# A two-block transformer kernel: linear heads in pairs on the two row halves, rotary queries of two heads in one unit, no engine barriers, early weight sums, idle products in the router

## The chip, the cores and the metric

One core of a Trainium2 chip. The metric is the device time of one execution in microseconds (us), lower is better. Everything is float32.

## What is computed

512 tokens of width 1024 pass two blocks.

Block one: a modulated norm and a gated feed-forward (width 2816), a mixer of 16 heads of 64 (8 stick-breaking, 8 softmax with forget gates and normalized queries and keys), and a second feed-forward.

Block two puts 16 meta tokens in front, so 528 positions:

```
z = rmsnorm(h) @ w_in                      # q, k, v, r, decay input, q_lat, kv_lat, k_rope
linear heads (4): chunks of 64 tokens; q_e = q exp(b), b = running sum of log decay in the chunk
   att = causal(q_e (k exp(-b))^T);  o = att v + q_e S;  S <- decay S + (k exp(b_last - b))^T v
   o <- o / rms(o) * gain * silu(r)
softmax heads (4): q = rmsnorm(q_lat) @ w_qb, 128 plain and 64 rotary values for each head
   scores = q k^T + rope(q_r) rope(k_r)^T, causal by chunk; softmax; times v
h <- h + concat(heads) @ w_out
router: one of 8 groups, in it the best 2 of 8 experts; h <- h + sum of gated expert outputs
```

The experts (64, of 6 MB each) end in a last norm.

## The kernel before

TensorE, VectorE (DVE), ScalarE (ACT) and SyncE (SP, which issues all transfers) each run one hand-ordered program; semaphores tie them. Weights come through six slots of 2 MB; `freed[s]` and `filled[s]` guard them. PSUM is eight banks.

**Barriers.** `phase_end` (L489) drains an engine and waits for all four; it stands ahead of both feed-forwards and of the second block (2, 8, 10). TensorE only reports there.

**Feed-forward** (`ffn`, L854, L897): each weight item goes through seven products of sums and differences of weights and tokens. Products one and two take plain weights and tokens; the third needs two weight sums (`gate_up_sum`, L1950 to L1962) and two token sums (`token_sum`, L1968 to L1977) of VectorE. VectorE makes the two weight sums of item 0 first, then two token sums, and so on (`ffn`, L2036). The token sums need the normed tokens that ScalarE scales (L1543).

**Mixer.** In the loop over heads TensorE turns the probabilities of head h (L977), makes scores of head h+1 (L968), the output of head h (`head_out`, L995) in bank 6, and half of a later pair's projections (`first_half` L944, `second_half` with `values` L950), whose banks are 6 and 7. Projections into bank 6 wait for `s_o`, the copy of the head's output by VectorE (L2170). The last two heads cover part of the output product, the rest (L1035) follows in eight tiles; VectorE adds each (L2231), ScalarE squares it (L1528), VectorE adds the squares (L1933).

**Norm of block two** (`norm(3)`): VectorE multiplies a tile with the inverse root (L1939), ScalarE with the gain (L1546), TensorE projects it (L1106).

**Linear heads.** Units (L1106 to L1120) project; `chunk_update` (L1156) makes the update of a chunk, VectorE the state (L2295). A head sits on 64 rows: heads 0 and 2 on the lower, 1 and 3 on the upper half. For each head in turn TensorE runs `gla_out` (L1177, then L1180 on the head's rows), `gla_scores` of the next head (L1163), and between them `mla_unit`s, three for each softmax head: query (L1197), rotary query (L1199, 64 columns), key (L1204). `gla_sum` (L1186) sums squares, ScalarE makes the inverse root (L1758, L1759), VectorE scales (L2310, L2311). VectorE turns the rotary queries (L2321 to L2326), masks scores (L2305). ScalarE copies plain queries and keys (L1747, L1749).

**Softmax heads.** 16 units, head by head, query tiles 0, 1, 2, 3. TensorE turns the probabilities of unit n (L1279, L1281), makes scores of n+2 (L1259 to L1262), then the output of n (L1291, L1293), which waits for ScalarE's copy of the turned tiles (L1779).

**Router and experts.** After the logits (L1318) VectorE picks experts in some 30 small steps while TensorE waits for `s_M`; two products (L1355, L1356) give ranks; VectorE norms the last rows (L2381, it stands ahead of the ranks' use) and marks the rows of the first four experts (L2434). `pick_first(b)` (L1373) gathers the rows of block b, ScalarE copies them (L1851), TensorE turns them (L1380), ScalarE copies (L1855), then `gate_up` (L1410) and `down` (L1430). SP issues in order: weights for block 3 when gate and up of block 0 are done (L707), a part of block 2 when down of block 0 is done (L741), then those of block 4, and so on in a loop.

`w_qb` is loaded by one transfer (L691) into slot 1, where `decay_product` (L1128) waits for it.

## Time and profile before

| | |
|---|---|
| median of 3 runs | 2441.39 us (2439.96 to 2443.12) |
| the profiled execution | 2439.12 us, span 2437.3 us |
| TensorE busy, granted clock | 89%, 0.957 |
| VectorE, ScalarE busy | 40%, 21% |
| moved from HBM | 546 MB, in the experts' part at 427 to 430 GB/s |

The span is the time between the first and last recorded instruction. PE is TensorE, PEld its weight loads; the clock is the share of full speed granted (0.50 is the 1.2 GHz level, 1.00 the 2.4 GHz one). One float32 matmul is two records. An idle time is followed by the instruction that ended it.

### The profile page before, as it was taken

Reading aid. Unit: us, or ns where it says so; the run is one execution under the profiler, and the core shown is the slowest. Engines: PE = TensorE matmul, PEld = TensorE weight load, DVE = VectorE, ACT = ScalarE, POOL = GpSimd, SP = SyncE. Lnnn points to the kernel's source line nnn. Section 1 sums busy time; section 2 is a strip of 40 time slices with the busy share of each in tenths; the row PEclk is TensorE's granted clock in tenths of the full one; section 3 lists DMA queues with packets and bytes.
Section 4 is the critical chain, followed back from the end, with each engine's and each line's share of the span. In section 5 each row is a group of like instructions: output and inputs, shape, how many; then the busy total and the mean of one; then the engine's idle time right before and its main releaser. Section 6 shows DMA issues by size and latency. Waiting matters only on the chain.

```text
span 2437.3 us, 34407 instructions
## 1 busy us (share of the span) xinstructions
PE 2158.9 (89%) x14427; PEld 1511.1 (62%) x14427; DVE 974.4 (40%) x1725; ACT 509.0 (21%) x1052; POOL 0.2 (0%) x4
## 2 busy tenths in 40 slices
PE   7999999999999999999999998777777777777776
PEld 4888888666564888888754554444444444444443
DVE  4777753145443543453223525322232222222223
ACT  3111100244323111110221422211111111111112
POOL 0000000000000000000000000000000000000000
PEclk9999999999999999999999999988998989998998
DMA  7565721411202224212401044999999999999997
GB/s 280 187 228 174 250 95 48 104 37 42 96 1 69 69 70 151 70 66 78 148 14 69 1 190 181 427 427 428 429 427 430 428 429 429 427 430 428 429 429 298
DMA packets 150550, 549.06 MB, mean 225 GB/s; under 512 B 9376, under 2 KB 102832, under 8 KB 124736
## 3 DMA queue, kind: packets, MB, share of 16 engines
q1 hardware_dynamic: 150464, 547.83, 57.1%
q8 instruction: 65, 1.06, 0.2%
q14 instruction: 21, 0.17, 0.0%
HBM read 545.71 MB, written 2.10 MB: 225 GB/s over the span
## 4 chain that ended last, share of the span: by engine, by line
PE 62%; DMA 30%; DVE 4%; ACT 1%; issue 1%; SPq 1%; ACTq 0%; PEldq 0%; DVEq 0%; PEld 0%
DMA slots<-in_expert_w_up 27%; PE ps L854 18%; PE ps L897 11%; PE ps L1410 8%; PE ps L944 4%; PE ps L1342 2%; PE ps L1035 2%; PE ps L1120 2%; PE ps L950 2%; DMA slots<-in_w_mod 2%; PE ps L968 1%; PE ps L1115 1%; PE ps L1118 1%; PE ps L977 1%; DMA slots<-in_expert_w_down 1%
## 5 line engine op out<-in xcount | busy, mean ns | idle before, releaser
L1410 PE MATMUL ps<-slots,xT 128*32 128x256 f32 x4032 | 292.8, 454 | 188.9 <-DMA slots<-in_expert_w_up 169.4
L1410 PEld LDWEIGHTS ps<-slots,xT 128*32 128x32 f32 x4032 | 158.3, 130 | 311.3 <-issue 176.8
L854 PE MATMUL ps<-hT,slots 128*128 128x256 f32 x1408 | 314.1, 381 | 6.5 <-ACT hT L1543 3.6
L854 PEld LDWEIGHTS ps<-hT,slots 128*128 128x128 f32 x1408 | 267.8, 191 | 46.5 <-ACT tmp L1564 4.5
L854 PE MATMUL ps<-slots 128*128 128x256 f32 x1056 | 238.0, 382 | 5.6 <-DVE slots L1972 5.6
L854 PEld LDWEIGHTS ps<-slots 128*128 128x128 f32 x1056 | 201.7, 192 | 33.8 <-issue 6.3
L2514 DVE COPY hT<-ps 128x128 f32<-128x128 f32 x64 | 18.5, 289 | 418.1 <-PE ps L1417 418.1
L2520 DVE TENSOR_TENSOR big<-ps,big 128x512 f32<-128x512 f32 x128 | 88.3, 691 | 219.0 <-PE ps L1445 219.0
L1831 ACT ACTIVATE xT<-ps 32x256 f32<-32x256 f32 x256 | 96.2, 376 | 259.5 <-PE ps L1430 257.3
L1430 PE MATMUL ps<-slots,hT 128*32 128x256 f32 x2040 | 123.3, 381 | 30.0 <-DVE hT L2514 29.5
L1825 ACT ACTIVATE big<-ps 32x256 f32<-32x256 f32 x128 | 48.0, 375 | 392.4 <-PE ps L1410 391.6
L1445 PE MATMUL ps<-xT,hT 128*128 128x512 f32 x256 | 123.5, 618 | 3.5 <-DVE big L2520 1.9
L897 PE MATMUL ps<-big,slots 128*128 128x256 f32 x528 | 116.6, 379 | 0.0
L1362 PEld LDWEIGHTS ps<-xT,big 128*128 128x128 f32 x960 | 108.3, 192 | 6.2 <-issue 6.2
L1362 PE MATMUL ps<-xT,big 128*128 128x128 f32 x960 | 111.2, 277 | 0.0
L897 PEld LDWEIGHTS ps<-big,slots 128*128 128x128 f32 x528 | 100.3, 190 | 13.6
L1430 PEld LDWEIGHTS ps<-slots,hT 128*32 128x32 f32 x2040 | 71.7, 109 | 58.1 <-issue 33.5
L944 PE MATMUL ps<-hT,slots 128*128 128x512 f32 x240 | 105.8, 596 | 0.0
L2033 DVE SCALAR_TENSOR_TENSOR xT<-ps,small,xT 128x256 f32<-128x256 f32 x56 | 27.0, 483 | 169.1 <-PE ps L897 169.1
L1445 PEld LDWEIGHTS ps<-xT,hT 128*128 128x128 f32 x256 | 39.5, 188 | 80.9 <-DVE big L2520 64.8
L1528 ACT ACTIVATE tmp<-xT 128x512 f32<-128x512 f32 (+1 forms) x32 | 20.2, 635 | 290.3 <-DVE xT L2033 254.5
L944 PEld LDWEIGHTS ps<-hT,slots 128*128 128x128 f32 x240 | 44.8, 190 | 54.6 <-issue 54.5
(381 smaller groups left out, 2562.1 us busy)
## 6 DMA issues: line engine op xcount, KB each, us to landing
slots<-in_expert_w_gate SPq DMA_DIRECT2D x63, 2048.0 KB, 18.4
slots<-in_expert_w_up SPq DMA_DIRECT2D x63, 2048.0 KB, 22.8
slots<-in_expert_w_down SPq DMA_DIRECT2D x63, 2048.0 KB, 24.7
slots<-in_w_mod SPq DMA_DIRECT2D x18, 2048.0 KB, 11.5
slots<-in_w_gate SPq DMA_DIRECT2D x22, 1024.0 KB, 5.5
slots<-in_w_up SPq DMA_DIRECT2D x22, 1024.0 KB, 8.1
slots<-in_w_down SPq DMA_DIRECT2D x8, 2816.0 KB, 10.2
slots<-in_w_in SPq DMA_DIRECT2D x24, 512.0 KB, 5.6
```

Of the source, the lines that this page charges most:

```text
L854: last = mm(bank[:, g], lhs[:, g, k], rhs[:, k], start=(first and g == 0 and k == 0), stop=(k == 3), skip_group_check=True)
L897: last = mm(bank, lhs[:, f], rhs[:, f], start=(first and f == 0), stop=(f == N_ITEM - 1), skip_group_check=True)
L944: last = mm(ps[:, bank, :], pair_w[p][:, k, m, :], hT[:, k, META:TOK], start=(k == 0), stop=(k == KC - 1))
L950: last = mm(ps[:, bank, t * P:(t + 1) * P], hT[:, k, META + t * P:META + (t + 1) * P], pair_w[p][:, k, 2, :], start=(k == 0), stop=(k == K ...
L1035: last = mm(ps[:, bank, :], wo[f // 4][:, f % 4, d * P:(d + 1) * P], oT[:, f, :], start=(f == f0), stop=(f == f1 - 1))
L1120: last = mm(ps[0:m, b, :], w2(it)[:, k, c0:c0 + m], hT[:, k, META:TOK], **flags)
L1362: last = mm(flat[:, 2048 + k * P:2048 + (k + 1) * P], u2[:, t, k * P:(k + 1) * P], hot[:, t, :], start=(t == 0), stop=(t == NT - 1))
L1410: last = mm(ps[at:at + CAP, j, 0:256], xsT[:, k, i * CAP:(i + 1) * CAP], w[g][k][:, 256 * h:256 * (h + 1)], start=(k == 0), stop=(k == KC ...
L1430: last = mm(ps[g * CAP:(g + 1) * CAP, 2 + j, 0:256], hid[j][:, c, :], w[c][:, g * 256:(g + 1) * 256], start=(c == 0), stop=(c == 3))
L1445: mm(ps[:, 4 + n % 2, :], gate_rows[:, n // 2, :], ys[:, n % 2 * 512:(n % 2 + 1) * 512], start=True, stop=True).then_inc(s_cmb, 1)
L1831: last = av(ys[i * CAP:(i + 1) * CAP, g * 256:(g + 1) * 256], ps[g * CAP:(g + 1) * CAP, 2 + i % 2, 0:256], ACT.Copy)
L2520: v.tensor_tensor(h2[:, t, g * 512:(g + 1) * 512], ps[:, 4 + g, :], h2[:, t, g * 512:(g + 1) * 512], ALU.add).then_inc(s_sum, 1)
```

## The change

- The barriers are gone.
- Mixer: head outputs go to bank 3; waits for head copies become waits for the copies that really share a bank, and a turn waits for the copy of the head before.
- The four weight sums of item 0 of the second feed-forward are made in the last four output tiles of the mixer.
- `norm(3)`: VectorE multiplies with root and gain at once, ScalarE does nothing.
- `w_qb` is laid out with all plain columns first, by four transfers; the rotary queries of two heads are one unit of 128 columns, 10 units in place of 12; tables and keys are doubled on the upper rows.
- Linear heads in pairs: matmuls of the two heads alternate; chunk updates too; two buffers each for masks, squares and roots.
- Query tiles of the softmax heads in the order 3, 0, 2, 1.
- Router: six products of 512 columns whose result nobody reads; the first rows of block 1 are picked after gate and up of block 0, those of block 2 after those of block 1.

In the diff, removed lines of the functions printed above are left out where a new version stands.

```diff
@@ -279,12 +278,12 @@
 o2 = hT[:, :, :].rearrange("p k t -> p (k t)")[:, 0:8 * SEQ].rearrange("p (c t) -> p c t", c=8)
-attS = eb[:, 0, :].rearrange("p (b c) -> p b c", b=4)
-osq = eb[:, 1, :]
-sil = tmp[:, 0, 0:SEQ]
-orst = tmp[:, 1, 0:SEQ]
+attS = [eb[:, j, :].rearrange("p (b c) -> p b c", b=4) for j in range(2)]
+osq = [extra[:, SEQ * j:SEQ * (j + 1)] for j in range(2)]
+sil = [extra[:, SEQ * (2 + j):SEQ * (3 + j)] for j in range(2)]
+orst = [extra[:, SEQ * (4 + j):SEQ * (5 + j)] for j in range(2)]
...
-qr = ring[0][0:ROPE, 2048:4096].rearrange("p (h t) -> p h t", h=GH)
+qr = ring[0][:, 2048:3072].rearrange("p (h t) -> p h t", h=GH // 2)
@@ -449,12 +448,13 @@
 def halves(ap):
...
-NU = 3 * GH
+MLA_PARTS = [(p, kind, 2 * p + j) for p in range(GH // 2) for kind, j in ((0, 0), (1, 0), (2, 0), (0, 1), (2, 1))]
+NU = len(MLA_PARTS)
...
 def mla_unit_out(n):
...
-    h, kind = n // 3, n % 3
-    return (s_mb, h + 1) if kind == 1 else (s_mtc, 2 * h + (1 if kind == 0 else 2))
+    p, kind, h = MLA_PARTS[n]
+    return (s_mb, p + 1) if kind == 1 else (s_mtc, 2 * h + (1 if kind == 0 else 2))
@@ -470,27 +470,18 @@
+MLA_UNITS = [(h, t) for h in range(GH) for t in (3, 0, 2, 1)]
...
 def mla_at(un):
-    return 1024 * (un % 2) + (512 - META if un % NT == NT - 1 else 0)
+    return 1024 * (un % 2) + (512 - META if MLA_UNITS[un][1] == NT - 1 else 0)
...
 def mla_z(un):
...
-    t = un % NT
+    _, t = MLA_UNITS[un]
...
-JOINED = (19, 22)
...
-def joined_count(n):
-    return 4 * (JOINED.index(n) + 1) if n > LAST_LEFT else 4
...
-def phase_end(eng, n):
...
-    eng.drain().then_inc(s_phase[min(n, LAST_LEFT + 1)], 1)
-    eng.wait_ge(s_phase[min(n, LAST_LEFT + 1)], joined_count(n))
@@ -686,9 +677,12 @@
         if n == 3:
-            sp.wait_ge(freed[1], u.take(1, 2)[1])
+            sp.wait_ge(freed[1], u.take(1, 5)[1])
...
-            sp.dma_start(w_qb, a["mla_w_qb_2"][0].rearrange("(k p) n -> p k n", p=P)).then_inc(filled[1], 16)
+            for k in range(2):
+                rows = a["mla_w_qb_2"][0][k * P:(k + 1) * P, :].rearrange("p (h n) -> p h n", h=GH)
+                sp.dma_start(w_qb[:, k, 0:GH * P].rearrange("p (h n) -> p h n", h=GH), rows[:, :, 0:P]).then_inc(filled[1], 16)
+                sp.dma_start(w_qb[:, k, GH * P:].rearrange("p (h n) -> p h n", h=GH), rows[:, :, P:]).then_inc(filled[1], 16)
@@ -970,6 +963,8 @@
     def turn(h):
         pe.wait_ge(s_p, h + 1)
+        if h:
+            pe.wait_ge(s_o, h + 1)
@@ -981,28 +976,19 @@
         pe.wait_ge(s_ptc, 2 * h + 2)
...
             for half, (q, k) in enumerate(two):
...
+                last = mm(ps[half * HD:(half + 1) * HD, 3, q * P:(q + 1) * P], vt[p % 2][:, k, lo:lo + HD],
...
+    def first_half(n):
...
             project(n, 1, 7, 0, 4)
...
+            if n > 1:
+                pe.wait_ge(s_vc, n)
@@ -1010,20 +996,23 @@
             project(n, 0, 7).then_inc(s_q, 1)
-            pe.wait_ge(s_o, heads + 1)
+            pe.wait_ge(s_vc, n)
...
-    def second_half(n, heads):
+    def second_half(n):
...
             mm(ps[:, 7, :], const("head_ones"), eb[:, 1, :], start=True, stop=True).then_inc(s_qss, 1)
-        pe.wait_ge(s_o, heads + 1)
+        if n < 4:
+            pe.wait_ge(s_qc, n + 1)
+        else:
+            pe.wait_ge(s_kc, n + 1)
@@ -1061,17 +1050,19 @@
         if h % 2 and p + 2 < N_PAIR:
-            first_half(p + 2, h + 1)
+            first_half(p + 2)
...
-            second_half(p + 1, h + 1)
+            second_half(p + 1)
...
                 bank = 7 - (d % 3) % 2
-                if bank == 6:
-                    pe.wait_ge(s_o, h + 2)
+                if bank == 6 and d == 1:
+                    pe.wait_ge(s_vc, N_PAIR)
+                elif bank == 6:
+                    pe.wait_ge(s_wp, 2)
@@ -1145,48 +1134,55 @@
...
+    def chunk_update(*chunks):
+        for n in chunks:
+            pe.wait_ge(*unit_out(U_GV + (n + 1) // 2))
+            if n == 0:
+                pe.wait_ge(s_ktc, 1)
+            if n >= 4:
+                pe.wait_ge(s_st, n - 3)
...
+            for n in chunks:
+                t, lo, rows = (0, 0, META) if n == 0 else (1 + (n - 1) // 2, (n - 1) % 2 * CHUNK, CHUNK)
+                last = mm(ps[:, 4 + n % 4, p * 256:(p + 1) * 256], kdtok[lo:lo + rows, t, p * P:(p + 1) * P],
+                          gv[lo:lo + rows, t, p * 256:(p + 1) * 256], start=True, stop=True)
+                if p:
+                    last.then_inc(s_U, 1)
...
+    def gla_scores(p):
+        if p:
+            pe.wait_ge(s_gstd, 2 * p)
...
+            for j in range(2):
+                last = mm(ps[:, 2 * j, b * P:(b + 1) * P], km[j * HD:(j + 1) * HD, p, META + b * P:META + (b + 1) * P],
+                          gq[j * HD:(j + 1) * HD, p, b * P:(b + 1) * P], start=True, stop=True)
+                if b == NT - 1:
+                    last.then_inc(s_at2, 1)
...
+    def gla_out(p):
+        if p == 0:
...
+        for j in range(2):
+            h = 2 * p + j
+            pe.wait_ge(s_atm, h + 1)
+            if p:
+                pe.wait_ge(s_gf, 2 + h - 1)
+            for b in range(NT):
+                mm(ps[:, 1 + 2 * j, b * P:(b + 1) * P], gv[:, 1 + b, h * P:(h + 1) * P], attS[j][:, b, :], start=(b == 0),
+                   stop=True, skip_group_check=True)
...
+            for j in range(2):
+                last = mm(ps[:, 1 + 2 * j, n * CHUNK:(n + 1) * CHUNK], states[j * HD:(j + 1) * HD, p, n + 1, :],
+                          gq[j * HD:(j + 1) * HD, p, n * CHUNK:(n + 1) * CHUNK], start=False, stop=True, skip_group_check=True)
+                if n == N_CHUNK - 1:
+                    last.then_inc(s_go, 1)
...
     def gla_sum(h):
         pe.wait_ge(s_gsq, h + 1)
...
+        mm(ps[:, 2 * (h % 2), :], ones, osq[h % 2], start=True, stop=True).then_inc(s_gss, 1)
...
     def mla_unit(n):
...
+        p, kind, h = MLA_PARTS[n]
@@ -1194,9 +1190,9 @@
             if kind == 0:
-                last = mm(ps[:, b, :], w_qb[:, k, h * 192:h * 192 + P], ql[:, k, :], start=(k == 0), stop=(k == 1))
+                last = mm(ps[:, b, :], w_qb[:, k, h * P:(h + 1) * P], ql[:, k, :], start=(k == 0), stop=(k == 1))
...
-                last = mm(ps[0:ROPE, b, :], w_qb[:, k, h * 192 + P:h * 192 + 192], ql[:, k, :], start=(k == 0), stop=(k == 1))
+                last = mm(ps[:, b, :], w_qb[:, k, (GH + p) * P:(GH + p + 1) * P], ql[:, k, :], start=(k == 0), stop=(k == 1))
@@ -1222,39 +1218,41 @@
     unit(U_GV + 2)
...
+    chunk_update(1, 2)
...
+    chunk_update(3, 4)
...
     pe.drain().then_inc(freed[ITEM_SLOT[1]], 1)
...
+    chunk_update(5, 6)
...
+    pe.wait_ge(*unit_out(U_GV + 4))
...
     mla_unit(1)
...
+    for p in range(2):
+        gla_out(p)
+        mla_unit(5 * p + 2)
+        mla_unit(5 * p + 3)
+        gla_sum(2 * p)
+        gla_sum(2 * p + 1)
+        mla_unit(5 * p + 4)
+        if p == 0:
+            mla_unit(5)
+            gla_scores(1)
+            mla_unit(6)
     def mla_value(t):
         pe.wait_ge(s_mtc, 8 if t < 2 else 8 + t - 1)
+        if t == 0:
+            pe.wait_ge(s_mb, GH // 2)
...
     def scores(un):
...
+        h, t = MLA_UNITS[un]
...
         q0 = t * P
...
+        for first, (lhs, rhs) in enumerate(((qn[:, h, q0:q0 + P], kn[h]), (qr[h % 2 * ROPE:(h % 2 + 1) * ROPE, h // 2, q0:q0 + P], kr[h % 2 * ROPE:(h % 2 + 1) * ROPE, :]))):
@@ -1350,6 +1348,8 @@
     pe.drain().then_inc(freed[3], 1)
+    for n in range(6):
+        mm(ps[:, n % 2, :], ident, ones.unsqueeze(1).to_broadcast([P, 4, P]), start=True, stop=True)
@@ -1447,14 +1447,15 @@
     def quad(q, start=False, end=False):
         if start:
+            pick_first(1)
...
-            pick_first(2)
...
         if start:
+            pick_first(2)
+            pick_first(3)
...
-            pick_first(3)
@@ -1484,7 +1485,6 @@
     pick_first(0)
-    pick_first(1)
@@ -1533,17 +1533,16 @@
     def norm_scaled(r):
+        if r == 3:
+            return
...
                 act.wait_ge(s_nx, normed_count(r, b, k))
...
+                av(rows, rows, ACT.Identity, scale=scale[r][:, k:k + 1],
+                   bias=modT[:, 24 * r + k:24 * r + k + 1]).then_inc(s_hn, 1)
@@ -1740,30 +1736,34 @@
     def mla_unit_copy(n):
...
+        _, kind, h = MLA_PARTS[n]
...
             av(halves(kn[h]), ps[:, b:b + 2, 0:264], ACT.Copy).then_inc(s_mtc, 1)
...
+    for p in range(2):
+        mla_unit_copy(5 * p)
+        for j in range(2):
+            act.wait_ge(s_go, 2 * p + j + 1)
+            av(osq[j], ps[:, 1 + 2 * j, :], ACT.Square).then_inc(s_gsq, 1)
+        mla_unit_copy(5 * p + 2)
+        mla_unit_copy(5 * p + 3)
+        for j in range(2):
+            act.wait_ge(s_gss, 2 * p + j + 1)
+            if p:
+                act.wait_ge(s_gf, 2 + j + 1)
+            link(av(orst[j], ps[:, 2 * j, :], ACT.Ln, scale=1.0 / P, bias=eps_col[:, 0:1]))
+            av(orst[j], orst[j], ACT.Exp, scale=-0.5).then_inc(s_gstd, 1)
+        mla_unit_copy(5 * p + 4)
     def mla_value(t):
...
     def mla_exp(un):
...
+        n = META + P * (MLA_UNITS[un][1] + 1)
+        act.wait_ge(s_mb, GH // 2 + un + 1)
@@ -1855,9 +1855,9 @@
     first_copied(0)
-    first_copied(1)
...
     gate_sigmoid(0, (0, 0))
+    first_copied(1)
@@ -1936,7 +1936,11 @@
             for k in range(KC):
-                v.tensor_tensor(hT[:, k, t0:t0 + w], xT[:, k, t0:t0 + w], rstd[:, t0:t0 + w], ALU.mult).then_inc(s_nx, 1)
+                if r == 3:
+                    v.scalar_tensor_tensor(out=hT[:, k, t0:t0 + w], in0=xT[:, k, t0:t0 + w], scalar=col("mix_norm_2", k),
+                                           in1=rstd[:, t0:t0 + w], op0=ALU.mult, op1=ALU.mult).then_inc(s_hn, 1)
+                else:
+                    v.tensor_tensor(hT[:, k, t0:t0 + w], xT[:, k, t0:t0 + w], rstd[:, t0:t0 + w], ALU.mult).then_inc(s_nx, 1)
@@ -2034,13 +2038,16 @@
     def ffn(r):
-        gate_up_sum(r, 0, 0)
-        gate_up_sum(r, 0, 1)
+        if r == 0:
+            gate_up_sum(r, 0, 0)
+            gate_up_sum(r, 0, 1)
...
         token_sum(r, 1)
-        gate_up_sum(r, 0, 2)
+        if r == 0:
+            gate_up_sum(r, 0, 2)
...
-        gate_up_sum(r, 0, 3)
+        if r == 0:
+            gate_up_sum(r, 0, 3)
@@ -2166,7 +2172,7 @@
     def head_copy(h):
...
         rows = oT[h % 2 * HD:(h % 2 + 1) * HD, h // 2, :].rearrange("p (q n) -> p q n", q=4)
-        out = ps[:, 6, :].rearrange("p (q n) -> p q n", q=4)
+        out = ps[:, 3, :].rearrange("p (q n) -> p q n", q=4)
@@ -2225,6 +2231,10 @@
     for j, k in enumerate(MIX_ORDER):
+        if j == 4:
+            dve.wait_ge(freed[3], 4)
+        if j >= 4:
+            gate_up_sum(1, 0, j - 4)
@@ -2232,11 +2242,9 @@
     norm(2)
-    phase_end(dve, 8)
...
     norm(3)
-    phase_end(dve, 10)
@@ -2266,7 +2274,8 @@
     link(v.tensor_tensor(swap[0:ROPE, :], swap[0:ROPE, :], const("rope_sin")[0:ROPE, :], ALU.mult))
-    v.tensor_tensor(kr[0:ROPE, :], kr[0:ROPE, :], swap[0:ROPE, :], ALU.add)
+    link(v.tensor_tensor(kr[0:ROPE, :], kr[0:ROPE, :], swap[0:ROPE, :], ALU.add))
+    v.tensor_copy(kr[ROPE:2 * ROPE, :], kr[0:ROPE, :])
@@ -2302,41 +2311,44 @@
     def gla_mask(h):
...
         dve.wait_ge(s_at2, h + 1)
...
+        v.tensor_tensor(attS[h % 2], ps[:, 2 * (h % 2), :].rearrange("p (b c) -> p b c", b=4),
...
     def gla_head(h):
         dve.wait_ge(s_gstd, h + 1)
...
+        link(v.tensor_tensor(sil[h % 2], gr[:, h, :], orst[h % 2], ALU.mult))
+        v.scalar_tensor_tensor(out=o2[:, h, :], in0=ps[:, 1 + 2 * (h % 2), :], scalar=col("gla_out_norm_2", h), in1=sil[h % 2],
...
+    def rope_queries(p):
+        n = 5 * p + 1
...
         dve.wait_ge(s_mz, n + 1)
...
+        if p:
+            dve.wait_ge(s_mb, p)
+        cos, sin = (const(c)[:, META:TOK] for c in ("rope_cos", "rope_sin"))
+        for lo in range(0, P, 32):
+            v.tensor_scalar(swap[lo:lo + 32, 0:SEQ], ps[lo ^ 32:(lo ^ 32) + 32, b, :], MLA_SCALE, None, ALU.mult)
+        link(v.scalar_tensor_tensor(out=qr[:, p, :], in0=ps[:, b, :], scalar=MLA_SCALE, in1=cos, op0=ALU.mult, op1=ALU.mult))
+        link(v.tensor_tensor(swap[:, 0:SEQ], swap[:, 0:SEQ], sin, ALU.mult))
+        v.tensor_tensor(qr[:, p, :], qr[:, p, :], swap[:, 0:SEQ], ALU.add).then_inc(s_mb, 1)
...
     gla_mask(0)
+    gla_mask(1)
...
+    rope_queries(0)
+    gla_head(0)
+    gla_head(1)
+    gla_mask(2)
+    gla_mask(3)
+    rope_queries(1)
+    gla_head(2)
+    gla_head(3)
...
     def mla_max(un):
...
+        _, t = MLA_UNITS[un]
```

## Rows read from the trace of the kernel before

**Rows 1.** The page, chain that ended last, share of the span by engine

```profile
PE 62%; DMA 30%; DVE 4%; ACT 1%; issue 1%; SPq 1%; ACTq 0%; PEldq 0%; DVEq 0%; PEld 0%
```

**Rows 2.** Windows: us, busy PE PEld DVE ACT POOL, clock, DMA share, GB/s; timeline, SP

```profile
1505.00:1510.00 5.00, 4.71 (x82) 2.68 (x86) 4.62 (x15) 1.22 (x4) 0.00 (x0) 1.00 0.13 23
...
1508.98 0.33 SPq L707 DMA_DIRECT2D slots<-in_expert_w_gate  x1
1520.26 0.33 SPq L741 DMA_DIRECT2D slots<-in_expert_w_down  x1
```

**Rows 3.** Timeline: start us, us, engine line op [idle before <-who ended it]; first feed-forward

```profile
44.62 1.23 DVE L1950 TENSOR_TENSOR slots<-slots 128x1024 f32<-128x1024 f32 x1 [5.86 <-ACTq L492]
49.71 6.50 PE L854 MATMUL ps<-slots 128*128 128x256 f32 x29 [2.06 <-DVE slots L1972]
```

**Rows 4.** Waits of TensorE in the mixer: total us, times, longest

```profile
PE ps L950 <- DVE big L2171: 3.5, 3, 1.2
```

**Rows 5.** Timeline, second feed-forward; chain, warm products; windows, the clock; timeline, last mixer tiles

```profile
792.28 1.22 DVE L1950 TENSOR_TENSOR slots<-slots 128x1024 f32<-128x1024 f32 x1 [3.27 <-ACTq L492]
...
797.38 9.89 PE L854 MATMUL ps<-slots 128*128 128x256 f32 x32 [3.53 <-DVE slots L1972]
...
88.38 17.28 PE ps L854 x80
...
798.00:800.00 2.00, 2.00 (x6) 1.62 (x5) 2.00 (x3) 0.00 (x0) 0.00 (x0) 0.50 0.00 0
...
776.96 0.75 DVE L2231 SCALAR_TENSOR_TENSOR xT<-ps,small,xT 128x512 f32<-128x512 f32 x1 [1.30 <-PE ps L1035]
```

**Rows 6.** Timeline, third norm: VectorE and ScalarE

```profile
1195.29 5.59 DVE L1939 TENSOR_TENSOR hT<-xT,rstd 128x264 f32<-128x264 f32 x16 [2.45 <-ACT rstd L1533]
1195.98 6.60 ACT L1546 ACTIVATE hT<-hT,cols 128x264 f32<-128x264 f32 x16
```

**Rows 7.** Timeline, linear heads: rotary unit and work, row halves, last outputs

```profile
1327.25 1.93 PE L1199 MATMUL ps<-big,slots 128*64 128x512 f32 x4 [1.45 <-DVE slots L2295]
1329.29 0.68 DVE L2321 TENSOR_SCALAR big<-ps 32x512 f32<-32x512 f32 x1 [2.10 <-PE ps L1199]
1331.59 0.37 PE L1163 MATMUL ps<-big,slots 64*128 64x128 f32 x1
1331.81 0.27 PE L1163 MATMUL ps<-big,slots 64*128 64x128 f32 x1
1331.81 0.27 PE L1180 MATMUL ps<-big,slots 64*128 64x64 f32 x1
...
1348.38 1.66 PE L1180 MATMUL ps<-big,slots 64*128 64x64 f32 x13
1350.86 0.49 PE L1204 MATMUL ps<-big,slots 128*128 128x264 f32 x1
...
1357.47 2.00 PE L1180 MATMUL ps<-big,slots 64*128 64x64 f32 x16
```

**Rows 8.** Waits of TensorE, softmax heads, 1361 to 1417

```profile
PE ps L1291 <- ACT big L1779: 2.4, 5, 0.9
```

**Rows 9.** Timeline, router and first experts

```profile
1495.80 1.98 DVE L2381 SCALAR_TENSOR_TENSOR big<-big,glst 128x1024 f32<-128x1024 f32 x1
1495.86 1.22 PE L1355 MATMUL ps<-hT,cst 128*128 128x256 f32 x2 [6.71 <-DVE hT L2423]
1499.00 5.45 PE L1373 MATMUL ps<-big 128*32 128x256 f32 x64 [1.06 <-DVE big L2434]
1509.25 1.93 PE L1373 MATMUL ps<-big 128*32 128x256 f32 x32
```

**Rows 10.** The DMA view, w_qb: size, us to landing; timeline, its issue and the waiting matmul

```profile
slots<-in_mla_w_qb SPq DMA_DIRECT2D x1, 768.0 KB, 8.4
...
1179.75 0.42 SPq L691 DMA_DIRECT2D slots<-in_mla_w_qb  x1
1211.00 2.04 PE L1128 MATMUL ps<-big,slots 16*128 16x264 f32 x8
```

128 lines of the change are left out of this document (9 added, 119 removed).

## The prediction

> **What bounds the kernel now.** I read the chain that ended last first. It is TensorE for 62% of the span and the experts' weight transfers for 30% [rows 1]. The chain in order of time passes through TensorE until about 1532 us and through transfers after that, so the question is whether time won ahead of the experts survives the transfer-bound part. It does if the stream of transfers is started by TensorE. The windows show the DMA engines at 0.13 between 1505 and 1510 [rows 2]: the stream stands still until the first expert's gate and up products free their slots at 1508.98, and once more waits for the first down product, whose end lets the next transfer go at 1520.26 [rows 2]. After that it is full. Everything that makes this down product earlier moves the end by as much. So I read the waits of TensorE stage by stage ahead of it; a stage without such waits can only gain where TensorE's own work shrinks.
>
> **The sum.** The profiled execution took 2439.12 us around a span of 2437.3 us; the median of the runs shown is 2441.39, 2.3 above it.
>
> 1. *Barrier ahead of the first feed-forward.* VectorE stands until ScalarE has scaled the last tile, then makes two weight sums of 1.23 us ahead of the two token sums; TensorE ends its two first products, sits 2.06 us and goes on behind the second token sum [rows 3]. Without the barrier the weight sums and the first token sum run during the scaling, and the second token sum, which needs the last scaled tile, ends about 1.2 us after it, at 45.8; TensorE's two products end at 47.65 and cover it. Gain 2.1.
>
> 2. *First attention.* Head outputs move from bank 6 to bank 3, so projections into bank 6 no longer wait for the copy of the head. That wait cost 3.5 us in three pieces, once per pair of the normalized heads [rows 4]. Everywhere else in this stage TensorE runs gapless, and the waits added (bank 3 free again before the next turn; bank 6 read by ScalarE) are for copies that ended microseconds before. What is next late there is the softmax, with over 2 us to spare. Gain 3.5. The 1.7 us that TensorE waits for a softmax at head 7 stay.
>
> 3. *Barrier and weight sums ahead of the second feed-forward.* Again VectorE starts behind ScalarE's last tile, and TensorE sits 3.53 us behind the second token sum [rows 5]. The four weight sums of 1.22 us move into the last output tiles of the attention, one per tile, where VectorE sits 1.30 us ahead of each tile [rows 5] and some more behind ScalarE's square: they fit, and their weights have landed by then. The second token sum then ends at 793.5, and TensorE's products at 793.8. The whole 3.53 goes. The clock goes with it: after the gap it is granted 0.50, the 1.2 GHz level, and 32 records take 9.89 us, where 80 take 17.28 warm, 0.216 each [rows 5]; with the last record's tail 32 would take 7.1. Without the gap this fall has no cause: 2.7 more. Gain 6.2. If only the gap goes it is 3.5.
>
> 4. *Third norm.* VectorE's own product now holds the gain, and the hop over ScalarE goes: ScalarE starts 0.69 after VectorE [rows 6], and the first projection starts as much earlier. VectorE's 0.35 per tile (16 in 5.59) stays under TensorE's 0.43 (two records of 0.216 [rows 5]). Gain 0.7. The barrier behind it ends while TensorE is in its first projection; nothing.
>
> 5. *Linear heads.* Before, this stretch is gapless on TensorE from 1327.25 to 1361.34, four rounds of 9.09 us. Its parts: a rotary unit is 4 records in 1.93, so 1.86 to the next [rows 7]; four become two: 3.7 less. Output and scores on row halves: 24 records take 2.48 (1348.38 to 1350.86), and the last head's 16 take 1.92 [rows 7], together 9.4 for the stretch. Records of the two lines, which sit on different row halves, start at the same 1331.81 [rows 7]: the halves run side by side. So 32 alternating output records should take what 16 take alone, 1.9, and 16 score records 0.95. For the stretch that is 4.75 in place of 9.4: 4.6 less. Pairing the chunk updates changes nothing, since those pairs already overlap. Against it stand three waits. The second mask (0.6) comes ahead of the last state on VectorE, and the first rotary unit waits for that state: 0.6. The rotary work on VectorE now has four swaps of 0.68 [rows 7] in place of two, 5 us for two heads; the next query unit, in the same bank, waits 0.15. At the end ScalarE makes the roots of both heads, two operations of 0.7 each (the length of the swap in [rows 7], and 512 columns like it), ahead of its last key copy, and the next matmul waits for that copy: by the order of the queues 1.6. Net: 3.7 + 4.6 + 0.2 (fewer handovers) - 0.6 - 0.15 - 1.6 = 6.2. Bounds: 2.5 if the halves overlap no better than now and the waits stay, 8 if no wait comes.
>
> 6. *Softmax heads in the order 3, 0, 2, 1.* TensorE waits five times for the turned probabilities, 2.4 us in all, three short ones and two at the end [rows 8]. The new order puts long scores beside the short units, so the three short waits (0.7) go, and the last unit is a short one: 0.2. Work is unchanged. Gain 0.9; bounds -1 (the exponentials of a long unit now stand ahead of a short unit's copies on ScalarE) and 1.7.
>
> 7. *Router.* TensorE waits 6.71 us for the router's choice [rows 9]. Six idle products of 512 columns, two records each at twice 0.216 [rows 5], fill 5.2 of it and should hold its clock. The rank products then run warm, but VectorE's 1.98 us row [rows 9] ends at 1497.8, hardly before the cold products did at 1498.0: 0.2. The first pick is the big one: 64 records take 5.45, the first 32 of them cold, and 32 take 1.93 warm [rows 9]. With the second pick moved behind the first gate products, these end near 1505.8 in place of 1508.98 [rows 2]. But the next point is the first down product. Between the two now stand, besides what stood there, one more pick (1.9) and the two copies of the second row that it no longer covers (1.0): 14.2 us in place of 11.3, so 1520.0 to 1520.1. The two transfers that start 3 us earlier only end 3 us earlier, into a longer hole. Gain 0.2, bounds 0 and 3.2 (if the stream is not held by that product).
>
> 8. *Weights of the rotary units.* One transfer of 3 KB rows becomes four of 512 and 256 B pieces on SP's queue, 2048 pieces. It was issued at 1179.75 and landed 8.4 us later; the first matmul that now waits for all of it starts at 1211.0 [rows 10]. 22.9 us hide it, and SP itself has 12 us until its next issue. Cost 0. The copy of the rotary keys to the upper rows is one more operation on VectorE, 0.7 like a swap of [rows 7], ahead of a key copy; VectorE waits for TensorE's key projection before that copy anyway. Bound 0.7, taken as 0.
>
> Sum: 2.1 + 3.5 + 6.2 + 0.7 + 6.2 + 0.9 + 0.2 = 19.8. From the profiled 2439.1 that gives 2419.3, from the median 2421.6.
>
> **A rule weighed.** One record of the output line starts at 1331.81, after one of the scores line at 1331.59 [rows 7], although all outputs are issued ahead of these scores: TensorE lets one row half run past the other. The Trainium skill (TensorE: Matmul & The Clock Gate, Part 3, The mechanism) says that matmuls keep the program's order in start and end. By that rule no score could have run inside an output, the stretch would hold 11.5 us of such records in place of 9.4, and pairing would give 6.7. The trace disagrees, and the 4.6 goes by the trace.
>
> **Rivals.**
> - *The pairs are held by VectorE and ScalarE* (13%). For: ScalarE's roots and VectorE's rotary work grow denser around each pair; my schedule leaves 0.15 us between rotary work and its bank. Against: both engines are idle half of the stretch. Item 5 then gives 2.5: 2425.3.
> - *The clock still falls in the second feed-forward* (10%), say because VectorE is late with a sum: 3.5 in item 3: 2424.3 or a bit more.
> - *The router's gain passes in full* (8%). The first restart at 1508.98 sets the stream: 3.0 more: 2418.6. Against: SP issues in order and its next transfer waits for the down product.
> - *The transfers hold the end anyway* (3%): 2441. Against: 0.13 [rows 2].
> - *Slower* (3%): the alternation between row halves does not overlap but drains. Place: the 96 output and score records and the 24 of the chunk pairs. If each record takes its full 0.27 (0.38 for an update), they cost 35 us against my 9: 26 more, 2447.8. It decides from about 0.24 us per record ((9 + 19.8) / 120). Against: the two records that start together [rows 7].
> - My sum as it stands: 63%.
>
> **Numbers.** Forecast 2421.6. Items 5 to 7 at their better ends give 2416, at their worse ones, with the clock rival, 2430; the profiled execution and the median lie 2.3 apart. Range 2415 to 2430. A difference of 0.2% (4.9 us) is about what a measurement of this kernel can tell from none. All cases but the last two are beyond it on the fast side: faster 0.94, same 0.03, slower 0.03.
>
> **What would show it.** Right: no wait of TensorE for a token sum in either feed-forward, and a granted clock of 1.00 ten microseconds after the second norm; no wait for head copies; about 27 us from the first rotary unit to the first value product, with one wait of 1 to 2 us at its end; gate products of the first expert 3 us closer to the last logits, the down product not; a longer hole in the transfers ahead of it. Wrong: output records of the linear heads more than 0.06 us apart on average, new waits of TensorE for VectorE's rotary work, or a stretch of half clock behind the longer idle time at the end of the linear heads.

## The result, and where it came from

The changed kernel takes 2421.78 us (median of four executions, 2420.56 to 2424.54) against 2441.55 for the kernel before: ratio 0.9918, 95% interval 0.9903 to 0.9932. That is 19.8 us, the forecast sum. A second measurement (five executions of it, nine of the kernel before) gave 2425.17 against 2442.43, ratio 0.9931 (0.9918 to 0.9945), 17.3 us. The profiled execution is the slowest of its four, 2424.54 us around a span of 2422.7. Medians are over the usual executions: one of the five of run e2 below took 3059.67 us, at a granted clock of 0.692, and is left out.

The total came out; several of its terms did not. The chain that ended last in the changed kernel (shares of the span), and TensorE's waits up to the router (total us, times, longest us):

```profile
PE 62%; DMA 30%; DVE 4%; ACT 2%; issue 1%; SPq 1%; PEldq 0%; PEld 0%; DVEq 0%; ACTq 0%
```

```profile
PE ps L848 <- ACT hT L1544: 3.6, 2, 2.0
...
PE ps L1195 <- DVE slots L2304: 2.0, 1, 2.0
...
PE ps L972 <- ACT big L1635: 1.9, 1, 1.9
...
PE ps L1248 <- ACT big L1745: 1.4, 1, 1.4
PE ps L848 <- DVE slots L1976: 1.4, 1, 1.4
PE ps L1289 <- ACT big L1779: 1.3, 2, 0.7
```

The chain has the shares that it had [rows 1], but for ScalarE's 2% instead of 1%. The wait for head copies [rows 4] is gone. The wait of 3.53 for a token sum [rows 5] is 1.4, the waits at the start and at the end of the linear heads are 2.0 and 1.4, and of the five for turned probabilities [rows 8] two are left.

Starts of TensorE's stretches, subtracted from each other, say where the time went. "Again" is a second profile of the same kernel (runs e8 and e1 below); "filled" is the fastest version found (e12).

| stretch | before, again | changed, again | forecast gain | filled |
|---|---|---|---|---|
| first feed-forward to first attention product | 416.60, 418.60 | 415.52, 413.98 | 2.1 | 415.72 |
| first attention to its last output block | 289.40, 289.40 | 290.42, 290.03 | 3.5 | 286.03 |
| second feed-forward and third norm | 411.67, 411.60 | 404.44, 404.44 | 6.2 + 0.7 | 404.39 |
| projections to the first rotary unit | 130.62, 130.64 | 131.34, 131.30 | -0.6 | 130.74 |
| linear heads, to the first value product | 34.09, 34.09 | 27.46, 27.46 | 6.8 | 26.95 |
| softmax heads, to the first output mix | 57.55, 57.55 | 55.72, 55.72 | 0.9 | 55.74 |
| output mixes and router, to the rank product | 76.97, 76.94 | 76.04, 76.04 | 0 | 76.04 |
| rank product to the transfer behind down(0) | 24.40, 24.40 | 23.59, 24.94 | 0.2 | 20.68 |

In the two profiled executions the gains add up to 1.1 - 1.0 + 7.2 - 0.7 + 6.6 + 1.8 + 0.9 + 0.8 = 16.8; the first product also starts 0.16 earlier, and 1520.26 [rows 2] becomes 1503.33. Of this 16.9, 14.6 are left in the span: the issues of the last output writes took 8.31 us instead of 7.15, and the rest lies in the expert transfers. That part varies by itself: from the rank product to the end of the span the kernel before took 941.4 us in one profile and 944.6 in the other, the changed one 943.0 and 942.1.

The second feed-forward, in the changed kernel and then before (start us, us, what, how many, idle time ahead of it):

```profile
784.74 7.26 PE L848 MATMUL ps<-hT,slots 128*128 128x256 f32 x32 [1.97 <-ACT hT L1544]
793.38 7.14 PE L848 MATMUL ps<-slots 128*128 128x256 f32 x32 [1.37 <-DVE slots L1976]
```

```profile
784.96 8.88 PE L854 MATMUL ps<-hT,slots 128*128 128x256 f32 x32 [1.98 <-ACT hT L1543]
```

The 32 records behind the gap take 7.14 us instead of 9.89 [rows 5], and those ahead of it 7.26 instead of 8.88: the clock had fallen before the gap as well.

The linear heads are as forecast. TensorE's timeline there:

```profile
1320.52 1.98 PE L1195 MATMUL ps<-big,slots 128*128 128x512 f32 x4 [2.05 <-DVE slots L2304]
1322.34 1.95 PE L1171 MATMUL ps<-eb,big 128*128 128x128 f32 x16
1324.22 2.00 PE L1175 MATMUL ps<-big,slots 64*128 64x64 f32 x32
...
1347.98 2.09 PE L1248 MATMUL ps<-slots,big 128*16 128x512 f32 x4 [1.43 <-ACT big L1745]
```

32 output records on alternating halves take 2.00 us where 16 of one head took 2.00 [rows 7]: 0.060 us each. At that spacing nothing is lost in the alternation.

The router: six idle products (12 records), rank product, first pick, and SP's issue behind down(0):

```profile
1473.54 5.41 PE L1352 MATMUL ps<-cst 128*128 128x512 f32 x12 [0.51 <-DVE hT L2387]
1479.74 0.70 PE L1355 MATMUL ps<-hT,cst 128*128 128x256 f32 x2 [0.79 <-DVE hT L2435]
...
1482.65 1.93 PE L1373 MATMUL ps<-big 128*32 128x256 f32 x32 [1.78 <-DVE big L2446]
...
1503.33 0.33 SPq L735 DMA_DIRECT2D slots<-in_expert_w_down  x1
```

The rank product takes 0.70 us instead of 1.22, and the first pick is warm [rows 9].

The attention is the surprise. It lost its waits for head copies and got no shorter. The timeline at the turn of head 7, and the windows there (us, then busy time of PE, PEld, DVE, ACT, POOL, granted clock, DMA share, GB/s):

```profile
609.58 1.67 PE L972 MATMUL ps<-cst,big 128*128 128x128 f32 x10 [1.89 <-ACT big L1635]
611.24 4.63 PE L961 MATMUL ps<-slots 72*128 72x128 f32 x8
615.80 2.40 PE L981 MATMUL ps<-big 128*64 128x128 f32 x20
```

```profile
605.00:610.00 5.00, 3.11 (x29) 2.92 (x28) 4.92 (x6) 1.74 (x2) 0.00 (x0) 1.00 0.17 38
610.00:615.00 5.00, 5.00 (x17) 3.13 (x15) 1.86 (x3) 0.83 (x2) 0.00 (x0) 0.54 1.19 316
615.00:620.00 5.00, 5.00 (x24) 2.84 (x23) 3.65 (x12) 2.15 (x8) 0.00 (x0) 0.50 1.02 406
```

The same records in the kernel before:

```profile
610.45 1.31 PE L977 MATMUL ps<-cst,big 128*128 128x128 f32 x10 [1.73 <-ACT big L1637]
612.10 2.43 PE L968 MATMUL ps<-slots 72*128 72x128 f32 x8 [0.34 <-DVE slots L2179]
614.46 1.31 PE L995 MATMUL ps<-big 128*64 128x128 f32 x20
```

TensorE waits for the softmax in both, 1.7 to 1.9 us. Behind that wait it ran at 2.4 GHz before and at 1.2 GHz in the changed kernel; 8 score records take 4.63 us instead of 2.43. The questions for the experiments were whether the edit causes this, whether it always happens, and what it costs to stop it.

### The profile page after: what moved, and what is told of

It reads as the page before. It is cut to its first block, busy times and chain, and to the rows that moved or that the text cites. A ratio compares the mean times of both kernels' runs of the same rounds, so it can differ in the third digit from the quotient of the medians.

```text
span 2422.7 us, 34395 instructions
## 1 busy us (share of the span) xinstructions
PE 2155.1 (89%) x14431; PEld 1503.0 (62%) x14431; DVE 971.5 (40%) x1720; ACT 501.3 (21%) x1036; POOL 0.2 (0%) x4
## 4 chain that ended last, share of the span: by engine, by line
PE 62%; DMA 30%; DVE 4%; ACT 2%; issue 1%; SPq 1%; PEldq 0%; PEld 0%; DVEq 0%; ACTq 0%
DMA slots<-in_expert_w_up 28%; PE ps L848 18%; PE ps L891 11%; PE ps L1410 8%; PE ps L937 4%; PE ps L1024 2%; PE ps L1109 2%; PE ps L1340 2%; PE ps L943 2%; PE ps L961 2%; DMA slots<-in_w_mod 1%; PE ps L1104 1%; PE ps L1107 1%; DVE acc L1920 1%; DVE rstd L1920 1%
## 5 line engine op out<-in xcount | busy, mean ns | idle before, releaser
L1410 PEld LDWEIGHTS ps<-slots,xT 128*32 128x32 f32 x4032 | 153.0, 131 | 318.4 <-DMA slots<-in_expert_w_up 179.3
```

The costliest lines, as they stand in the source:

```text
L1410: last = mm(ps[at:at + CAP, j, 0:256], xsT[:, k, i * CAP:(i + 1) * CAP], w[g][k][:, 256 * h:256 * (h + 1)], start=(k == 0), stop=(k == KC ...
```

## The experiments

Stretches are those of the table. Runs e4 to e10 are one execution each, and the five of e1 spread over 4.8 us, so these runs are read by their stretches and not by their times. "Lost to the clock" is an estimate: in windows of 2 us, TensorE's busy time times what the granted clock lacks to 1.00, added up from 30 to 1530 us.

**e1_again: the changed kernel, unedited.**

> The changed kernel once more, to see which of its stretches repeat. In the profiled execution the first attention took as long as before, though its waits for head copies were gone (3.5 us): at the turn of head 7 TensorE waited 1.89 us for the softmax and the granted clock was then 0.50 to 0.54 from 610 to 620 us, where the kernel before waited 1.73 us and kept 1.00. Theory A (the fall belongs to the shape of this stretch): it is there again, and from the first attention matmul (455.1) to the last block of the output product (745.5) pass 290.4 us. Rival B (chance of one execution): no fall, 287 us. The same question for the first feed-forward, where 32 matmul records took 9.04 us at a granted clock of 0.55 to 0.59 and 7.9 before: A 9.0 again, B 7.2 to 8. Median as before, 2420 to 2424.

Median 2425.17 (2422.51 to 2427.27). The fall at head 7 is there again:

```profile
609.71 1.31 PE L972 MATMUL ps<-cst,big 128*128 128x128 f32 x10 [1.89 <-ACT big L1635]
611.37 4.53 PE L961 MATMUL ps<-slots 72*128 72x128 f32 x8 [0.34 <-DVE slots L2185]
```

Attention 290.03. The fall in the first feed-forward is not: 32 records took 7.88 us, the stretch 413.98, 2.6 less than before. In its place 1.6 us are lost at 454 to 458 and 1.4 in the first pick. So in these two profiles A holds at head 7 and B in the first feed-forward.

**e2_idle_at_head7: two idle products in the wait.**

```diff
 def turn(h):
-    pe.wait_ge(s_p, h + 1)
     if h:
         pe.wait_ge(s_o, h + 1)
+    if h == 7:
+        for _ in range(2):
+            mm(ps[:, 3, :], ident, ones.unsqueeze(1).to_broadcast([P, 4, P]), start=True, stop=True)
+    pe.wait_ge(s_p, h + 1)
```

> The changed kernel with two idle products of 512 columns on TensorE ahead of the turn of head 7, in the 1.89 us in which it waits for the softmax (two take 1.8 at the 0.90 that each of the six in the router took). Theory A (the idle time of TensorE brings the clock down): granted clock 1.00 from 605 to 625, the 8 score records after the turn take 2.4 instead of 4.63 and the output records 1.3 instead of 2.4; attention 3.4 us shorter (290.4 to 287.0), median 3 to 4 below the unchanged one of this call. Rival B (the fall comes from something else, such as the weight transfers that start at 610): clock 0.5 from 610 to 620 as before, nothing gained. Rival C (chance): no fall in either kernel.

```profile
607.39 1.98 PE L969 MATMUL ps<-cst 128*128 128x512 f32 x4
609.21 1.28 PE L975 MATMUL ps<-cst,big 128*128 128x128 f32 x10
610.83 2.43 PE L961 MATMUL ps<-slots 72*128 72x128 f32 x8 [0.34 <-DVE slots L2188]
613.18 1.31 PE L984 MATMUL ps<-big 128*64 128x128 f32 x20
```

The clock held; the attention took 285.91 us, 4.1 less than in e1 (where 1.6 were lost at its start too) and 3.5 less than before: the forecast gain. B falls, since the same transfers were running (DMA share 1.16 from 610 to 615). C does not fall by this run alone: e4 below keeps the clock with the wait left empty. The median is 2422.48, 2.7 below e1 where 3 to 4 were expected, and in the profiled execution (2423.74) the rank product came at 1480.11 instead of 1478.59. Other waits lost the clock in this execution: 1.7 us at 780, 1.7 at 1316 and 4.5 at 1394 to 1406; softmax heads and mixes took 58.40 and 77.59.

**e3_down_first: the first down product ahead of the picks.**

```diff
     gate_up(1, q, start=start)
-    if start:
-        pick_first(2)
-        pick_first(3)
-        turn_first(2)
-    else:
+    if not start:
         combine(before(q))
     turn_hidden(0)
     down(0, q)
     if start:
+        pick_first(2)
+        pick_first(3)
+        turn_first(2)
         turn_first(3)
```

> The changed kernel with the first down product issued right behind the gate and up products of the second expert, ahead of the row picks of experts 2 and 3, which then stand behind it. The prediction held that the stream of expert transfers is set by the end of this down product, not by the gate and up products that end 3.2 us earlier in the changed kernel. If so: the down product starts near 1497.8 instead of 1501.35, its transfer is issued near 1499.8 instead of 1503.33 (3.5 earlier), the hole in the transfers ahead of it closes by as much, and the median falls by 3 to 3.5. Rival (the next transfers then wait for the third expert's products, which start 1.4 us later): the gain is given back at the transfer that waits for the second down product, 0 to 1 us left. Rival (something else holds the stream): 0.

The transfer is issued 20.67 us after the rank product instead of 23.59, 2.9 earlier where 3.5 were expected. The hole ahead of it, in the windows of the changed kernel and then of this one:

```profile
1500.00:1505.00 5.00, 4.53 (x68) 2.82 (x71) 3.76 (x8) 1.95 (x6) 0.00 (x0) 1.00 0.43 134
```

```profile
1500.00:1505.00 5.00, 4.25 (x72) 2.74 (x64) 1.92 (x5) 1.67 (x5) 0.00 (x0) 1.00 0.88 324
```

From 4 to 200 us behind the rank product 80.84 MB are moved instead of 79.79: at 428 GB/s 2.5 us. The next transfer, behind the second down product, is issued 1.7 later and costs little: at the last transfer of up weights 2.1 us of the gain are left (884.56 against 886.70 us behind the rank product). Median 2420.29, 4.9 below e1, though the rows give 2.1 to 2.5; the intervals of the two ratios overlap (0.9899 to 0.9930 and 0.9918 to 0.9945), so the difference of the medians is not shown to be larger. The forecast's rule holds for the restart: the transfers resume with the end of this down product.

**e4_linear_order: two orders in the linear heads.**

```diff
 gla_mask(0)
-gla_mask(1)
 state(N_CHUNK - 1)
+gla_mask(1)
@@ ScalarE, behind the root of the pair's first head
+                    if j == 0:
+                        mla_unit_copy(5 * p + 4)
-                mla_unit_copy(5 * p + 4)
```

> The changed kernel with two orders altered in the linear heads: VectorE makes the last state ahead of the mask of head 1, and ScalarE makes the last key copy between the roots of heads 2 and 3 instead of behind both. By the theory that both waits come from the order of the queues, TensorE waits 1.4 instead of 2.05 us for the state ahead of the first rotary unit, and 0.6 to 0.8 instead of 1.43 for the key copy ahead of the first value product; first rotary unit to first value product 26.7 us instead of 27.46, both together 1.3 us earlier. Rival (the next operation of the same engine then comes late: the mask for the outputs, or the root for the last head): new waits of the same size, 0. This run leaves the attention and the router as they are, so it is also another look at the clock there.

The waits are 1.45 and 0.70, as expected, with a new one of 0.22 for a root; the linear heads take 26.95 and the stretch ahead of them 130.75 instead of 131.3: 1.1 together, where 1.3 were expected (time 2423.08). And it shows that the fall at head 7 is not fixed:

```profile
609.76 1.31 PE L972 MATMUL ps<-cst,big 128*128 128x128 f32 x10 [1.89 <-ACT big L1635]
611.42 2.42 PE L961 MATMUL ps<-slots 72*128 72x128 f32 x8 [0.34 <-DVE slots L2186]
```

The same 1.89 us of waiting, no edit in the attention, and no fall: 286.80 us. Most of the time saved there was lost behind the softmax heads (windows as above):

```profile
610.00:620.00 10.00, 9.66 (x50) 5.54 (x49) 7.50 (x20) 3.15 (x10) 0.00 (x0) 1.00 1.10 358
1394.00:1406.00 12.00, 10.90 (x35) 7.06 (x36) 1.25 (x3) 1.55 (x3) 0.00 (x0) 0.72 0.49 183
```

**e5_late_sums: the early weight sums undone.**

```diff
-                if j == 4:
-                    dve.wait_ge(freed[3], 4)
-                if j >= 4:
-                    gate_up_sum(1, 0, j - 4)
@@ ffn(r): the four sums for r == 1 too, where they were
```

> The changed kernel with VectorE's four weight sums of the second feed-forward back behind the norm, ahead of and between the token sums; the barrier stays away. In the changed kernel TensorE waits 1.37 us for the second token sum (792.00 to 793.23 on VectorE), which starts when ScalarE has scaled the last tile at 791.97. Theory (the barrier alone made the 3.5 us wait): VectorE is free from 788.8 on, makes its first two weight sums and the first token sum by 792.5 and the second token sum by 793.7, so TensorE waits 1.8 instead of 1.37 and the early sums were worth 0.5 us. Rival (the early sums carry this gain): the wait is back at 3 to 3.5 us, and the clock falls behind it as before (9.9 us for 32 records). Also another look at the clock at the turn of head 7.

```profile
781.82 7.27 PE L848 MATMUL ps<-hT,slots 128*128 128x256 f32 x32 [1.98 <-ACT hT L1544]
790.86 7.14 PE L848 MATMUL ps<-slots 128*128 128x256 f32 x32 [1.78 <-DVE slots L1976]
```

The wait is 1.78 us and the clock stays. The barrier made most of the 3.5 us; the early sums are worth 0.4 (404.84 against 404.44; time 2423.87).

**e6_heads_apart: the pair one head after the other.**

```diff
-                for n in range(N_CHUNK):
-                    for j in range(2):
+                for j in range(2):
+                    for n in range(N_CHUNK):
@@ and likewise in the scores
```

> The changed kernel with the two linear heads of a pair issued one after the other instead of alternating: 4 + 4 score records and 16 + 16 output records on one row half and then on the other. The pair that alternates takes 2.00 us for 32 output records (0.060 us each) and the 16 before them of one half took 1.92 (0.11 each). Theory (records on different row halves run side by side only when they are near each other in the program): 32 output records take about 3.7 us, 1.7 more for each pair and 3.5 to 4 for the stretch. Rival (TensorE takes the next half's records ahead of the order whatever the distance): 2.0 to 2.5. First rotary unit to first value product 27.46 in the changed kernel: 30.5 to 31.5 by the theory, at most 28.5 by the rival.

```profile
1336.27 1.95 PE L1171 MATMUL ps<-eb,big 128*128 128x128 f32 x16
1338.15 3.76 PE L1175 MATMUL ps<-big,slots 64*128 64x64 f32 x32
1341.84 2.13 PE L1200 MATMUL ps<-big,slots 128*128 128x264 f32 x4
```

```profile
1330.00:1338.00 8.00, 8.00 (x45) 5.44 (x43) 5.58 (x9) 3.08 (x6) 0.00 (x0) 1.00 0.00 0
1338.00:1348.00 10.00, 10.00 (x44) 6.86 (x44) 3.32 (x5) 2.39 (x4) 0.00 (x0) 0.66 0.00 0
```

32 records take 3.39 and 3.76 us (0.11 each) instead of 2.00, the second 16 scores 1.71 instead of 1.16: 3.7 in all. The halves overlap when their records alternate, and hardly at all when 16 output or 8 score records of one stand ahead of the other's; nothing between was tried. The stretch took 33.04 (time 2428.19); most of the rest is a fall of the clock: windows of 1 us show 1.00 up to 1341 and 0.50 to 0.51 from there to 1347. It came at the end of the second 32 records, and the records that it slowed are mostly full-width ones. TensorE had not been idle since 1318.67, and behind the first such 32 records, at 1325.7, the clock stayed. The rule weighed in the prediction (the Trainium skill, TensorE: Matmul & The Clock Gate, Part 3, The mechanism) has matmuls start and end in program order. These times agree with it, and the 2.00 us do not go against it, since there the neighbours in the program sit on different halves and can keep their order. What disagrees is only the order of a few starts where two lines meet [rows 7].

**e7_softmax_order: the tiles in the order 0, 1, 2, 3.**

```diff
-        MLA_UNITS = [(h, t) for h in range(GH) for t in (3, 0, 2, 1)]
+        MLA_UNITS = [(h, t) for h in range(GH) for t in range(NT)]
```

> The changed kernel with the softmax heads' tiles back in the order 0, 1, 2, 3. The order 3, 0, 2, 1 gave 1.83 us from the first value product to the first output mix (57.55 to 55.72), by the rows 1.06 of it in waits for the turned probabilities and 0.8 in a clock that fell behind the last two waits before. Theory: five waits of together 2.4 us are back, 56.8 without and 57.5 with the fall of the clock. Rival (the stretch gained elsewhere, by the paired rotary queries): 55.7 to 56.

56.80 us (time 2421.56), and the five waits are back as they were [rows 8]:

```profile
PE ps L1289 <- ACT big L1779: 2.4, 5, 0.9
```

The order is worth 1.08; the other 0.75 of 1.83 goes with the fall behind the heads, which e7 does not have.

**e8_before_again: the kernel before, unedited.**

> The kernel before once more, to see which falls of the clock repeat in it. In its profiled execution the granted clock was below 1.00 behind the 3.5 us wait of the second feed-forward (4.4 us lost with the time ahead of it), at 1416 to 1422 (1.6) and at 1492 to 1504 behind the router's wait of 6.7 us (2.9), 8.9 us in all; the attention had none. Theory (waits above 3 us always bring it down, waits of 1 to 2 us in some executions): the first and the last of these are there again, the middle one or another of its kind may or may not be; at the turn of head 7, where it waits 1.7 us, either. Rival (all falls belong to the program): the same list again.

Time 2443.94. All three falls are there again (1.6 and 2.7, 1.6, and 2.9 us), and one more of 1.7 at 50 to 54, behind the 2.05 us wait of the first feed-forward: 10.5 lost against 8.9. The attention has none. Two profiles can't tell the theory from its rival for the middle one, which stands behind waits of 0.9 and 0.8 us.

**e9_no_idle_router and e10_old_picks: the two halves of the router's edit.**

```diff
@@ e9
-            for n in range(6):
-                mm(ps[:, n % 2, :], ident, ones.unsqueeze(1).to_broadcast([P, 4, P]), start=True, stop=True)
@@ e10
             pick_first(0)
+            pick_first(1)
             turn_first(0)
             gate_up(0, (0, 0), False, start=True)
@@ quad
-                    pick_first(1)
                     turn_first(1)
+                    pick_first(2)
@@ quad, behind gate_up(1)
-                    pick_first(2)
-                    pick_first(3)
                     turn_first(2)
+                    pick_first(3)
@@ and ScalarE's first_copied(1) moved ahead in the same way
```

> The changed kernel without the six idle products in the router. Theory (they hold the clock, no more): the two rank products take 1.2 and 1.06 us again instead of 0.70 and 0.59, the rank sum on VectorE ends 0.2 later, and the first pick of 32 records takes 3.4 instead of 1.93; rank product to the transfer behind the first down product 25 us instead of 23.6. Rival (the clock is back by then whatever was done): 23.8.

> The changed kernel with the row picks in their former order (0 and 1 ahead of the first gate products, 2 ahead of the second, 3 behind it), the idle products kept. Forecast step: the new order brings the first gate and up products 3 us forward but leaves the first down product where it is, 0.2 us. In the traces the transfer behind that product is issued 23.59 us after the rank product, 24.40 before, and the stream of transfers stands 1.1 to 2.0 us earlier after it. Theory (the order itself gives nothing at the down product; a warm pick gives 1.5): 22.3 to 23.0 us here, and by the end of the stream the two orders differ by the 1.2 us that the earlier restart saves. Rival (the order carries the gain): 24.0 to 24.4.

| | order of picks | idle products | rank product to transfer | MB moved from 4 to 200 us after the rank product |
|---|---|---|---|---|
| before | old | no | 24.40 | 79.32 |
| e9 | new | no | 25.88 | 78.78 |
| e10 | old | yes | 22.38 | 80.23 |
| changed | new | yes | 23.59 | 79.79 |
| e3 | new, down first | yes | 20.67 | 80.84 |

```profile
1481.86 3.66 PE L1373 MATMUL ps<-big 128*32 128x256 f32 x64 [1.78 <-DVE big L2446]
...
1501.33 0.33 SPq L735 DMA_DIRECT2D slots<-in_expert_w_down  x1
```

The rows are e10's: 64 pick records take 3.66 instead of 5.45 [rows 9]. The idle products alone give 2.0 us at the transfer; the new order takes 1.2 of it back. Both first theories hold at the transfer (25.88 where I said 25, since the whole first pick ran at the lower clock in 3.64 us). What I added for e10 is wrong: the order's earlier restart of the stream saves nothing, e10 has moved 0.44 MB more, 1.0 us. Two limits. The idle products do not always hold the clock: behind them, at the 1.8 us wait ahead of the first pick, it fell in e1, e4 and e5, and there the transfer came at 24.94 to 25.22. And further on the lead melts: the last transfer of up weights is issued 886.64 us behind the rank product in e10 and 886.70 in the changed kernel, and from the rank product to the end of the span pass 943.3 us in e9 (time 2424.15), 942.5 in e10 (2423.17) and 943.0 and 942.1 in the changed kernel. The two halves are shown at the transfer, not at the end.

**e11_orders and e12_orders_idle: the orders together, and idle products in the other waits.** e11 is e3 with e4. e12 adds to it:

```diff
+            def idle(bank, n, w=4):
+                for _ in range(n):
+                    mm(ps[:, bank, 0:w * P], ident, ones.unsqueeze(1).to_broadcast([P, w, P]), start=True, stop=True)
@@ ahead of the second feed-forward's first wait
+                    idle(5, 2)
@@ ahead of the first attention product
+            idle(7, 2)
@@ unit 0, behind the third norm
+                    idle(2, 1)
@@ turn(7)
+                    idle(3, 2)
@@ second MLA unit
+                        idle(1, 1)
@@ the last two softmax units
+                    idle(2 * (un % 2), 1, 2)
@@ first pick
+                    idle(4, 1)
```

> The changed kernel with the three orders altered that shortened a stretch by themselves: the first down product ahead of the picks (2.9 us earlier by its rows, 2.5 us at 200 us into the stream), and the two of the linear heads (27.46 to about 26.9, and the first rotary unit 0.6 earlier). Expected 3.5 to 4 us below the changed kernel, 2417.5 to 2421 on this chip, where the unchanged one gave 2425.2; less if the clock falls in more places.

> The same, and idle products in TensorE's waits of 1.2 to 2 us: two ahead of the first attention and of the second feed-forward, one behind the third norm, two at the turn of head 7, one ahead of the first rotary unit, a half one at each of the last two softmax units, one ahead of the first pick. Theory (each such wait brings the clock down in some executions, 5 to 8 us per execution in all of the changed kernel's profiles): the sum of what is lost below full clock before the experts falls to under 2 us, the median by 3 to 5 against the run with the orders alone. Rival (the falls are of the chip's own making and move elsewhere, as one did when the wait at head 7 was filled): 5 us or more are lost all the same, and the medians agree within 2 us. Rival (idle products hold up the real ones): slower by up to 1.

e11: 2420.78 (2419.31 to 2424.24), ratio 0.9916 (0.9901 to 0.9930), 4.4 below e1 and inside the expected 2417.5 to 2421. e12: 2414.77 (2413.53 to 2417.87), ratio 0.9886 (0.9871 to 0.9902), the fastest of all and 6.0 below e11, where 3 to 5 were expected. Lost to the clock: 6.2 us in e11, 1.7 in e12, and those at 40 to 46, behind the wait ahead of the first feed-forward, which was left empty. That accounts for 4.5 of the 6.0. The windows of e11 and then of e12:

```profile
610.00:620.00 10.00, 9.66 (x50) 5.54 (x49) 7.50 (x20) 3.16 (x10) 0.00 (x0) 1.00 1.10 358
1394.00:1406.00 12.00, 10.90 (x32) 6.97 (x33) 1.25 (x3) 1.55 (x3) 0.00 (x0) 0.58 0.50 182
```

```profile
610.00:620.00 10.00, 9.66 (x51) 5.54 (x51) 7.53 (x19) 3.28 (x10) 0.00 (x0) 1.00 1.09 356
1394.00:1406.00 12.00, 11.33 (x45) 6.45 (x44) 1.66 (x4) 1.56 (x3) 0.00 (x0) 1.00 0.64 228
```

The theory holds in this one profile: with these waits filled, the clock is not lost anywhere else, though waits of 1.4 (the second token sum) and 0.7 us are still there. The executions without a timeline fit: the slowest of the four of e12 is faster than the fastest of the five of e11, and their mean granted clock is 0.961 to 0.963 against 0.959 to 0.961. e11 did not get below e3 in the median, though its rows are 1.1 us shorter; it lost 6.2 us to the clock and e3 5.1.

**All profiles together.** Of the ten profiles of changed kernels in which the wait at head 7 is left empty, six lose the clock there (changed, e1, e3, e5, e6, e7) and none of these at 1394 to 1406; the other four (e4, e9, e10, e11) keep it at head 7 and all lose it at 1394 to 1406. The attention then takes 286.8 instead of 289.2 to 290.4. These four have another fall, of 1.6 us, at 454 to 460; against the 285.91 of e2, which has neither, the fall at head 7 by itself cost 3.3 (e5, e7) to 4.5 us (changed, e3). Whether the edit brought it is not shown: the two profiles of the kernel before have none, and nor have four of these ten. In e10, 57.11 and 77.66 for the two stretches behind it stand against 55.72 and 76.04, 3.0 given back.

## Why the prediction was right, and where it was not

The forecast of 2421.6 and the range were met, and the case "my sum as it stands" is nearest. Term by term:

1. *Barrier ahead of the first feed-forward, 2.1.* Right without a fall of the clock: 1.8 to 2.6 in the ten profiles that have none there, 1.1 in the profiled execution, where the granted clock was 0.57 from 40 to 44. The step "TensorE's two products end at 47.65" took the clock of before for granted. The stretch of before varies too (416.60, 418.60).
2. *Attention, 3.5.* The mechanism is right (the waits are gone, and e2 gives 3.5), the term failed. The step was "the 1.7 us that TensorE waits for a softmax at head 7 stay": it stayed, but I priced it as idle time and not as a place where the clock can go. It cost about 3 to 4.5 us in six of ten profiles.
3. *Second feed-forward, 6.2.* With the third norm 7.2 against 6.9. The split was wrong: the gap shrank by 2.2 and not by 3.5, since the second token sum ended at 793.23, near the forecast 793.5, but TensorE's first two products, now at full clock, end at 792.0 and not at 793.8; the clock gave 4.4 instead of 2.7. Early sums 0.4 (e5).
4. *Third norm, 0.7.* Right: TensorE waits 1.2 us instead of 1.9.
5. *Linear heads, 6.2 net.* Measured 6.6 - 0.7 = 5.9. The two waits were forecast as 0.6 more and 1.6 and are 0.6 more and 1.4; e4 confirms the causes of the waits and e6 the overlap. The 4.6 for the pairing was 4.4: two lines of 32 outputs in 1.93 each and one of 16 scores in 1.09, 4.95 us instead of 9.4. The argument beside it was weaker than it looked. The 11.5 us "by that rule" count 96 records at 0.12, but the stretch of before held 88 (the first eight scores stand ahead of it), most of them 0.107 apart, and only two pairs of starts fall together where an output line meets the next scores. That saves about 0.2 us at each of three such places, so without any overlap the stretch would hold about 10.0 (an estimate from these rows). The row in [rows 7] showed that the halves can run side by side; before, they hardly did.
6. *Softmax order, 0.9.* 1.08 for the order (e7). The 0.8 of the clock behind the heads, and 0.9 more in the first mixes, stood nowhere in my sum: they come with the fall at 1416 to 1422 of before.
7. *Router, 0.2.* 0.8 at the down product, about 1.1 in the stream (79.79 against 79.32 MB at 428 GB/s); at the end of the span it can't be told from the spread of that part. The rule "the stream waits for the down product" held at the restart (e3). Mis-sized was the sum of two effects of opposite sign: the idle products are worth 2.0, the order -1.2 (e9, e10). I credited the warm picks to the earlier gate products and then let the down product lose all of it.
8. *Weights in four pieces, 0.* TensorE has no wait for a transfer in that stage.

In the profiled execution items 1 and 2 fell short by 5.5 us and item 5 by 0.3, and 3, 6, 7 and the mixes gave 2.8 more: 16.8 instead of 19.8. That the medians lie 19.8 apart in one measurement and 17.3 in the other says that the forecast is at the upper end of what the change gives, and that its exact hit is in part luck. Of the rivals, "the clock still falls" was the right kind at the wrong place: it did not fall in the second feed-forward, where I had looked. The pairs were not held, the transfers did not hold the end, and the slower case needed 0.24 us per record where they take 0.06; of "the router's gain passes in full", 0.8 of 3.0 passed.

## What to carry to other kernels

A wait of 1 to 2 us of TensorE can bring its clock down in one execution and not in the next, and what an edit gained elsewhere can be paid back there: price such a wait as its idle time and, in some executions, 1.5 to 5 us more. Filling these waits with idle products of about their length cost nothing that the rows show and took 4.5 us of losses away; six such products ahead of the router's ranks were worth 2 us at the next transfer, more than the reordering that came with them. Read gains by the starts of stretches in several profiles: one profile of each kernel would have called the attention edit worthless.

## What had not been expected of the hardware

- The same wait (1.89 us), with the attention's program unchanged, is followed by a granted clock of 0.50 to 0.54 or of 1.00, and which one goes with whether a later stretch, 790 us on, keeps its clock. Why it goes with that was not settled: the profiles that lose it at 1394 to 1406 have their first value product at 1342.5 to 1344.2, those that don't at 1345.4 or later. No run shifted the program by a chosen amount.
- The clock fell behind waits of 0.7 and 0.6 us (at 1394 to 1406), and in e6 with no wait in the 22 us ahead, at the end of 32 records that used one row half at a time. The Trainium skill (TensorE: Matmul & The Clock Gate, HAM oscillation) puts the falls down to long idle gaps; the runs show them after short ones as well.
- Records of 64 rows overlap across the halves when they alternate in the program and hardly when one half's line stands ahead of the other's: 0.060 us each against 0.11.
- Idle products did not delay the work behind them when they fit: the rank product of the filled version still waits 0.79 us for VectorE behind the six, and the attentions with the wait at head 7 filled are the two shortest measured (285.91, 286.03).
